# Norm weights asked for ahead of the inputs, input tiles scaled ahead of older norms, a weight unit in its own buffer, and a second home for the bias of odd head pairs

## The chip, the cores and the metric

The kernel runs on one core of one Trainium2 chip. The metric is the device time of one execution, in microseconds (us); lower is better. Engines: PE (TensorE), DVE (VectorE), ACT (ScalarE), POOL (GpSimd), SP (SyncE, which here only issues transfers). ACT issues transfers too.

## The reference

One step of a two-layer decoder over 8 sample tokens and a prompt of 1024 tokens, model width 1024, everything in float32. Cut to what matters here:

```python
h = rms_norm(x, norm_mix[0])                    # x * rsqrt(mean(x^2) + eps) * gain
z = h @ w_in                                    # (1032, 1024) @ (1024, 3080)
qa, ka = rms_norm(z_q), rms_norm(z_k)           # per head of 64, 8 heads
logf = log_sigmoid(z_f + b_f)
qb, kb = partial_rope(rms_norm(...), pos)       # second group of 8 heads
c = cumsum(logf)
s = q @ k.T * SCALE + (c_q - c_k), causal       # heads 0..7: bias of the forget gate
s = q @ k.T * SCALE, three dilated windows      # heads 8..15
o = softmax(s) @ v
x = x + concat(o) @ w_out
x = x + swiglu(rms_norm(x)); x = x + gmlp(rms_norm(x)); x = x + swiglu(rms_norm(x))
```

## The kernel before

The engines' programs are written out by hand, each in the order in which its engine runs it, and tied by semaphores. Nothing is reordered by a scheduler.

**Split products.** A float32 product is made of three fast ones: each matrix is split into a high part, rounded (`Wh`, `Xh`), and a remainder (`Wl`, `Xl`), and PE computes high by high, high by low and low by high. Weights come in units of 128 partitions by 1024 values: a unit is loaded into one of two buffers `raw` (`load_unit`), rounded to `Wh` and its remainder subtracted to `Wl` (on POOL in `split_unit`, on ACT and POOL in `round_unit` and `remainder_unit`), into one of six slots. `split_done` counts the units whose split is done, and the load of unit n waits until unit n - 2 is split, since it takes that unit's buffer.

**Input projection, first pass.** The 1032 tokens lie in nine tiles: tile 0 has the 8 sample tokens, tiles 1 to 8 have 128 each. The pass over layer 0's first group makes three column blocks c = 0, 1, 2 (queries, keys, values), each from four weight units; for each tile, PE does 24 matmuls of 512 columns (`wide_products`, lines 527 to 529). During block 0 the input tiles are also prepared, each through this chain:

- SP loads the tile (`load_input`, line 2095, four buffers `xs`); PE transposes it with eight matmuls (`input_transpose`, line 547); ACT squares it and sums the squares (`input_square`, line 573).
- DVE multiplies the transposed tile by the norm weights `gains` into one of two buffers `hx` (`input_scale`, lines 604 and 607).
- ACT rounds it to `Xh` (`input_high`, line 586) and copies the transposed input to `xT` (`input_copy`, line 580); POOL, for tiles 0 and 1 DVE, subtracts the remainder `Xl` (`input_low`, line 558).

Two tiles are prepared before the loop. In the loop, step tt prepares tile tt + 3 (`inputs_behind`; step 0 prepares tiles 2 and 3). In the same step DVE finishes the norm and rotary part of the products of tile tt: a sum over squares made by ACT (line 752), a reciprocal after ACT's root (lines 691 and 758), two multiplications (761, 764) and four small rotary operations (770, 771, 772, 774). ACT stores tile tt - 1 before it goes on with step tt (`in_store`, line 669), which makes it wait for DVE's last operation on that tile.

The four units of block 0 are loaded by ACT into `raw[0]`, `raw[1]` and two more buffers `raw_first[2]`, `raw_first[3]`; ACT rounds them (line 706) and POOL subtracts (line 2168). Unit 4 (the forget gate's) and unit 5 are split by POOL between input tiles, units 6, 7 and 8 are rounded by ACT (line 382) in step 7 and finished by POOL (line 387). Block 1 begins with units 5 to 8.

**Attention.** Eight pairs of heads, eight query tiles each (units of work; the longest first, `unit(u)`), the steps numbered u. Pairs 0 to 3 add a bias row read from memory (`bias`, 128 partitions by 2 heads by 1024 values), pairs 4 to 7 a constant `dist` in the same place. PE computes scores, DVE adds the bias and takes the row's least value (line 1357), ACT takes the exponential (1274), PE transposes (1160) and multiplies by the values (1188). A row longer than 512 is done in two chunks: columns 512 up first, then columns 0 to 511. PE's `spread_sums` (line 1172) needs DVE's reciprocal of a step (line 1365), which stands behind the second chunk of the unit ahead. The bias of the next pair is loaded by ACT in three parts, issued at steps 2, 4 and 6 of a pair (`load_bias`, lines 1002 and 1004): columns 512 to 1023, 256 to 511, 0 to 255, each as soon as the last reader of these columns of the old pair is done. In between, keys and values of the sample tokens are streamed through `kring` and `ring`, and DVE sums their products (line 1384).

After attention come the output projection, two feed-forward stages and the gated layer, all bound by PE's matmuls.

Of the kernel before, what the change touches and what calls it, by code (L numbers as in the profile page):

```python
# [13 lines left out]
P = 128  # L14
# [20 lines left out]
RAW = 2  # L35
# [57 lines left out]
def build(nc, a):  # L93
    with ExitStack() as ctx:
# [32 lines left out]
        xT = place("xT", [P, KT, T])  # L127
        Xh = place("Xh", [P, KT, T], F32R)
# [130 lines left out]

        used[0] = lfp_memory  # L260
# [29 lines left out]
        raw_first_in = sems("raw_first_in", 2)  # L290
        xt_ps, xt_act = sem("xt_ps"), sem("xt_act")
# [86 lines left out]
        def round_unit(act, n):  # L378

            wait_released(act, n - SPL)  # L380
            act.wait_ge(raw_in[n % RAW], raw_value(n, n))
            act.activation(Wh[n % SPL][:, :], raw[n % RAW][:, :], ACT.Copy).then_inc(split_high, 1)

        def remainder_unit(pool, n):

            pool.wait_ge(split_high, n + 1)
            pool.tensor_tensor(Wl[n % SPL][:, :], raw[n % RAW][:, :], Wh[n % SPL][:, :].bitcast(F32),  # L387
# [128 lines left out]
        def wide_products(pe, n0, s0, tt, bank, first, final):  # L516
# [3 lines left out]
            for k in range(KT):  # L520
                if first and k % 2 == 0:

                    pe.wait_ge(split_done, n0 + k // 2 + 1)
# [64 lines left out]
        def input_act(act, tt):  # L588
            input_high(act, tt)
# [81 lines left out]
        def in_act(act):  # L671
            def step(i):
                for c in range(3):
                    for tt in range(TT):
# [46 lines left out]
        def in_dve(dve):  # L721
            def step(i):
                for c in range(3):
                    if is_first(i) and c == 2:
                        forget_sums_out(dve)
                    for tt in range(TT):
# [14 lines left out]
                        if c == 2:  # L741
# [6 lines left out]
                            continue  # L748
                        dve.wait_ge(z_squared, n + 1)
# [247 lines left out]
        def load_bias(eng, it, part):  # L997
# [1302 lines left out]
```

## Time and profile before

| | us |
|---|---|
| median of 3 runs | 2718.53 (2715.62 to 2722.75) |
| the profiled execution | 2714.44 |
| its span in the profile | 2712.6 |
| PE busy | 2604.7 (96%) |
| DVE busy | 1142.4 (42%) |
| POOL busy | 1114.5 (41%) |
| ACT busy | 547.0 (20%) |
| mean granted TensorE clock | 0.984 |

How to read it: the profile shows one execution. A row of the timeline gives the start, the duration, the engine, the line of the kernel, the operation, what it writes and reads, how often, and in brackets how long the engine had been idle and what ended that. The clock is given as a share of 2.4 GHz.

### The profile page before, as it was taken

How to read it: one execution, taken by the hardware profiler on the slowest of the kernel's cores; microseconds unless marked ns; L12 is line 12 of the kernel's file. 1: busy time of each engine (PE TensorE's matmuls, PEld its weight loads, DVE VectorE, ACT ScalarE, POOL GpSimd, SP SyncE). 2: the span in 40 equal slices, each digit the busy share in tenths (PEclk: the TensorE clock that was granted, in tenths of full speed). 3: DMA queues.
4: the chain of work that ended last, by engine and by line, in shares of the span. 5: the costliest groups of instructions: out<-in, count | busy, mean ns of one | idle time of the engine just before them, and what ended most of it. 6: DMA issues, size and time to landing. Idle time of an engine off the chain costs nothing.

```text
span 2712.6 us, 43122 instructions
## 1 busy us (share of the span) xinstructions
PE 2604.7 (96%) x16505; PEld 2366.2 (87%) x16505; DVE 1142.4 (42%) x2249; ACT 547.0 (20%) x1247; POOL 1114.5 (41%) x714
## 2 busy tenths in 40 slices
PE   7999988998899999999999998998999999999999
PEld 5777755565699999999999986798999999999999
DVE  6636536566516333333333342334533333333333
ACT  5201135565413000000000042311210000000001
POOL 5225115455566433333333254416553333333330
PEclk9999999999999999999999999999999999999999
DMA  5223147575411111111111101101021111111111
GB/s 147 74 77 87 56 123 220 175 215 177 129 55 47 55 47 46 46 46 46 46 46 46 39 32 47 48 16 55 20 67 47 46 46 46 46 46 46 46 31 63
DMA packets 220765, 189.86 MB, mean 70 GB/s; under 512 B 29571, under 2 KB 173443, under 8 KB 220644
## 3 DMA queue, kind: packets, MB, share of 16 engines
q1 hardware_dynamic: 200996, 161.89, 20.4%
q10 hardware_dynamic: 19648, 26.35, 2.7%
q8 instruction: 77, 1.26, 0.2%
q14 instruction: 44, 0.36, 0.0%
HBM read 171.19 MB, written 17.01 MB: 69 GB/s over the span
## 4 chain that ended last, share of the span: by engine, by line
PE 66%; DVE 4%; POOL 1%; ACT 1%; issue 1%; ACTq 0%; POOLq 0%; DVEq 0%
PE ps L495 62%; DVE hs L454 1%; PE ps L527 1%; PE ps L528 1%; PE ps L529 1%; POOL acc_sq L425 1%; ACT ps L1938 1%; DVE Xl L2013 0%; DVE acc_sq L446 0%; PE ps L1913 0%; DVE Xl L468 0%; POOL Xl L468 0%; POOL Wl L387 0%; DVE VM_LATE L2026 0%; PE ps L2050 0%
## 5 line engine op out<-in xcount | busy, mean ns | idle before, releaser
L495 PE MATMUL ps<-Xh,Wh 128*128 128x256 f32 (+2 forms) x2712 | 875.4, 323 | 16.7 <-DVE Xl L2013 6.3
L495 PE MATMUL ps<-Xl,Wh 128*128 128x256 f32 (+2 forms) x2712 | 869.4, 321 | 0.0
L495 PE MATMUL ps<-Xh,Wl 128*128 128x256 f32 (+2 forms) x2712 | 868.0, 320 | 0.0
L373 POOL TENSOR_TENSOR Wh<-raw,zeros 128x1024 fp32r<-128x1024 f32 x178 | 353.3, 1985 | 1076.4 <-PE ps L495 790.1
L495 PEld LDWEIGHTS ps<-Xh,Wh 128*128 128x128 f32 x2712 | 512.2, 189 | 22.9 <-issue 9.5
L495 PEld LDWEIGHTS ps<-Xl,Wh 128*128 128x128 f32 x2712 | 512.0, 189 | 1.2 <-issue 0.6
L495 PEld LDWEIGHTS ps<-Xh,Wl 128*128 128x128 f32 x2712 | 512.5, 189 | 0.0
L376 POOL TENSOR_TENSOR Wl<-raw,Wh 128x1024 fp32r<-128x1024 f32 x178 | 439.2, 2467 | 14.0
L1729 DVE TENSOR_TENSOR Hl<-hf,Hh 128x392 fp32r<-128x392 f32 (+1 forms) x132 | 180.6, 1368 | 466.1 <-ACT Hh L1657 466.1
L495 PE MATMUL ps<-Hh,Wh 128*128 128x392 f32 (+2 forms) x1056 | 341.5, 323 | 2.5 <-DVE xT L1738 2.5
L495 PE MATMUL ps<-Hl,Wh 128*128 128x392 f32 (+2 forms) x1056 | 338.6, 321 | 0.0
L495 PE MATMUL ps<-Hh,Wl 128*128 128x392 f32 (+2 forms) x1056 | 337.4, 319 | 0.0
L1738 DVE TENSOR_TENSOR xT<-ps,xT 128x392 f32<-128x392 f32 (+2 forms) x528 | 262.9, 513 | 168.7 <-PE ps L495 165.7
L1649 ACT ACTIVATE sg<-ps 128x392 f32<-128x392 f32 (+1 forms) x132 | 60.6, 459 | 1068.3 <-PE ps L495 1068.3
L527 PE MATMUL ps<-Wh,Xh 128*128 128x512 f32 (+1 forms) x576 | 231.2, 401 | 22.0 <-ACT VM_EARLY L1929 5.3
L529 PE MATMUL ps<-Wh,Xl 128*128 128x512 f32 (+1 forms) x576 | 229.5, 398 | 0.0
L528 PE MATMUL ps<-Wl,Xh 128*128 128x512 f32 (+1 forms) x576 | 229.1, 398 | 0.0
L1727 DVE TENSOR_TENSOR hf<-ps,sg 128x392 f32<-128x392 f32 (+1 forms) x132 | 67.2, 509 | 324.6 <-PE ps L495 320.5
L495 PEld LDWEIGHTS ps<-Hh,Wh 128*128 128x128 f32 x1056 | 199.6, 189 | 3.5 <-DVE xT L1738 3.2
L495 PEld LDWEIGHTS ps<-Hh,Wl 128*128 128x128 f32 x1056 | 200.2, 190 | 0.0
L495 PEld LDWEIGHTS ps<-Hl,Wh 128*128 128x128 f32 x1056 | 200.1, 190 | 0.0
L1089 POOL TENSOR_TENSOR kring<-kring,qrep 128x512 f32<-128x512 f32 (+1 forms) x96 | 120.8, 1274 | 110.5 <-DMA qrep<-q_sample 48.0
(213 smaller groups left out, 2482.2 us busy)
## 6 DMA issues: line engine op xcount, KB each, us to landing
raw<-in_w_gate_up SPq DMA_DIRECT2D x88, 512.0 KB, 3.8
raw<-in_w_down SPq DMA_DIRECT2D x44, 512.0 KB, 3.5
kring<-in_cache_a_k SPq DMA_DIRECT2D x64, 256.0 KB, 3.7
ring<-in_cache_a_v SPq DMA_DIRECT2D x64, 256.0 KB, 3.4
raw<-in_w_in_even SPq DMA_DIRECT2D x21, 512.0 KB, 4.0
raw<-in_w_in_c SPq DMA_DIRECT2D x16, 512.0 KB, 3.9
xs<-in_x_prompt SPq DMA_DIRECT2D x8, 512.0 KB, 5.7
q_prompt<-zt ACTq DMA_DIRECT2D x16, 256.0 KB, 2.0
```

The costliest lines, as they stand in the source:

```text
L373: pool.tensor_tensor(h[:, :], r[:, :], zeros[:, :].to_broadcast([P, 1024]), ALU.add).then_inc(split_high, 1)
L376: pool.tensor_tensor(l[:, :], r[:, :], h[:, :].bitcast(F32), ALU.subtract).then_inc(split_done, 1)
L425: pool.tensor_tensor(acc_sq[b][:, 0:n], sq[t % 2][:, 0:n], other, ALU.add).then_inc(s["summed"].sem, 1)
L495: ins = nc.tensor.matmul(out, w, x, start=(j == 0), stop=(j == len(pairs) - 1))
L527: nc.tensor.matmul(out, xh, h, start=(k == 0), stop=False)
L528: nc.tensor.matmul(out, xh, l, start=False, stop=False)
L529: last = nc.tensor.matmul(out, xl, h, start=False, stop=(k == KT - 1))
L1089: pool.tensor_tensor(keys, keys, qrep[0:r, g, :], ALU.mult).then_inc(prod_done, 1)
L1649: act.activation(sg[:, k % NB, 0:w], ps[:, gate_bank(i, is_last, k), 0:w], ACT.Silu).then_inc(f["silu"].sem, 1)
L1727: dve.tensor_tensor(hf[:, k % NB, 0:w], ps[:, bank, 0:w], sg[:, k % NB, 0:w], ALU.mult).then_inc(f["hid"].sem, 1)
L1729: dve.tensor_tensor(Hl[:, t, c0:c0 + w], hf[:, k % NB, 0:w], Hh[:, t, c0:c0 + w].bitcast(F32), ALU.subtract).then_inc(f["low"].sem, 1)
L1738: dve.tensor_tensor(x, ps[:, jobs.index(("dn", b, m, 0)) % 6, 0:w], x, ALU.add).then_inc(f["dn_add"].sem, 1)
```

## The change

In words: (1) SP asks for the first norm weights before input tile 1, not after it. (2) At the start, DVE does tile 0 whole, then the remainder of weight unit 1 (POOL did that), then tile 1; ACT rounds tile 0 and unit 1 before it squares tile 1, and unit 2 before it rounds tile 1. (3) In the loop, DVE scales the coming input tile before it sums the squares of tile tt, and ACT rounds that input tile before the root. (4) The load of unit 5 and of unit 8 moves ahead of input tiles 6 to 8, and unit 8 goes into `raw_first[2]`, so that it no longer waits for unit 6. (5) The bias of pairs 1 and 3 lies in `bias_odd`, in memory of `Xh` that is free until pair 4 writes it; so the bias of each further pair, or `dist`, is loaded in one piece at step 2.

```diff
+        bias_odd = nc.alloc_sbuf_tensor_at("bias_odd", [P, 2, SEQ], F32, offset=(xh_memory + 31) // 32 * 32 + 4 * T * (KT // 2))
...
         def round_unit(act, n):
 
             wait_released(act, n - SPL)
-            act.wait_ge(raw_in[n % RAW], raw_value(n, n))
-            act.activation(Wh[n % SPL][:, :], raw[n % RAW][:, :], ACT.Copy).then_inc(split_high, 1)
+            if n == 8:
+                act.wait_ge(raw_first_in[0], 32)
+            else:
+                act.wait_ge(raw_in[n % RAW], raw_value(n, n))
+            act.activation(Wh[n % SPL][:, :], early_home(n)[:, :], ACT.Copy).then_inc(split_high, 1)
...
         def input_act(act, tt):
-            input_high(act, tt)
             input_copy(act, tt)
...
+                        behind = inputs_behind(tt) if is_first(i) and c == 0 else ()
+                        for t in behind[:-1]:
+                            input_high(act, t)
+                            input_act(act, t)
+                        for t in behind[-1:]:
+                            input_high(act, t)
                         if c < 2:
                             act.wait_ge(z_sum, n + 1)
...
-                        if is_first(i) and c == 0:
-                            for t in inputs_behind(tt):
-                                input_act(act, t)
+                        for t in behind[-1:]:
+                            input_act(act, t)
...
             input_square(act, 0)
             round_first(0)
-            input_square(act, 1)
             input_high(act, 0)
             round_first(1)
+            input_square(act, 1)
+            round_first(2)
             input_high(act, 1)
-            round_first(2)
             round_first(3)
...
+                        if is_first(i) and c == 0:
+                            for t in inputs_behind(tt):
+                                input_scale(dve, t)
+                            if tt == 0:
+                                dve.wait_ge(const_in, 16 * CONSTS)
                         dve.wait_ge(z_squared, n + 1)
...
-                        if is_first(i) and c == 0:
-                            for t in inputs_behind(tt):
-                                input_scale(dve, t)
                         dve.wait_ge(z_root, n + 1)
...
             input_scale(dve, 0)
+            input_low(dve, 0)
+            dve.wait_ge(split_high, 2)
+            dve.tensor_tensor(Wl[1][:, :], raw_first[1][:, :], Wh[1][:, :].bitcast(F32), ALU.subtract).then_inc(unit1_low, 1)
             input_scale(dve, 1)
-            input_low(dve, 0)
             input_low(dve, 1)
-            dve.wait_ge(const_in, 16 * CONSTS)
...
-            positive_wait(eng, s_biased, 2 * chunk_base[max(8 * (it - 1) + (4, 6, 8)[part], 0)])
+        def load_bias(eng, it):
+
+            positive_wait(eng, s_biased, 2 * chunk_base[8 * (it - 1)])
             if it < PAIRS // 2:
-                eng.dma_start(bias[:, :, lo:hi], c_dram[2 * it:2 * it + 2, lo:hi].partition_broadcast(P)).then_inc(bias_in[part], 16)
+                eng.dma_start(bias_home(it)[:, :, :], c_dram[2 * it:2 * it + 2, :].partition_broadcast(P)).then_inc(bias_in[0], 16)
...
-                    if j in (2, 4, 6):
-                        load_bias(act, it + 1, (j - 2) // 2)
+                    if j == 2:
+                        load_bias(act, it + 1)
...
                 sp.dma_start(ident[:, :], a["c_ident"]).then_inc(ident_in, 16)
-                load_input(1)
                 sp.dma_start(gains[:, 0, :], a["norm_mix"][0].rearrange("(m p) -> p m", p=P)).then_inc(gain_in, 16)
-                load_input(2)
-                load_input(3)
+                for tt in range(1, NX):
+                    load_input(tt)
...
             load_unit(sp, BASE_FG, BASE_FG, rows(a["w_in_even"], 0, KT, 3 * DH, P), KT)
+            load_unit(sp, 5, 5, rows(a["w_in_even"], 0, 2, DH, DH), 2)
+            with nc.allow_non_contiguous_dma("512-byte and longer runs"):
+                sp.dma_start(raw_first[2][:, :].rearrange("p (a b) -> p a b", a=2), rows(a["w_in_even"], 6, 2, DH, DH)).then_inc(raw_first_in[0], 16)
             for tt in range(6, TT):
                 load_input(tt)
...
-            for n in range(4):
+            for n in (0, 2, 3):
 
                 pool.wait_ge(split_high, n + 1)
+                if n == 3:
+                    pool.wait_ge(unit1_low, 1)
+                pool.tensor_tensor(Wl[n][:, :], raw_first[n][:, :], Wh[n][:, :].bitcast(F32), ALU.subtract).then_inc(
+                    split_done, 2 if n == 2 else 1)
```

How the order moves, at three places. First ACT before the loop (`hx_117` belongs to even tiles, `hx_118` to odd ones; `Wh_65` to `Wh_68` are weight units 0 to 3). Before:

```order
L573 ACTIVATE hx_117,ssx<-xs_88 8x1024
L706 ACTIVATE Wh_65<-raw_63 128x1024
L573 ACTIVATE hx_118,ssx<-xs_89 128x1024
L586 ACTIVATE Xh<-hx_117 128x8x8
L706 ACTIVATE Wh_66<-raw_64 128x1024
L586 ACTIVATE Xh<-hx_118 128x8x128
L706 ACTIVATE Wh_67<-raw_first_115 128x1024
L706 ACTIVATE Wh_68<-raw_first_116 128x1024
```

ACT before the loop now:

```order
L585 ACTIVATE hx_117,ssx<-xs_88 8x1024
L722 ACTIVATE Wh_65<-raw_63 128x1024
L598 ACTIVATE Xh<-hx_117 128x8x8
L722 ACTIVATE Wh_66<-raw_64 128x1024
L585 ACTIVATE hx_118,ssx<-xs_89 128x1024
L722 ACTIVATE Wh_67<-raw_first_115 128x1024
L598 ACTIVATE Xh<-hx_118 128x8x128
L722 ACTIVATE Wh_68<-raw_first_116 128x1024
```

The square of tile 1, which needs tile 1's transfer, moved behind the first two units.

Second, DVE in step 1 of block 0, before (`zsq` are the squares of tile 1's products, `hx_117` is input tile 4):

```order
L752 TENSOR_REDUCE ss<-zsq_96 128x8
L604 TENSOR_SCALAR eps_ms<-ssx 128x1
L607 TENSOR_TENSOR hx_117<-ps,gains 128x1024
L758 RECIPROCAL zrs<-zstd 128x8
L761 TENSOR_TENSOR zt_93<-ps,zrs 128x512
```

DVE in the same step now:

```order
L615 TENSOR_SCALAR eps_ms<-ssx 128x1
L618 TENSOR_TENSOR hx_117<-ps,gains 128x1024
L773 TENSOR_REDUCE ss<-zsq_96 128x8
L776 RECIPROCAL zrs<-zstd 128x8
L779 TENSOR_TENSOR zt_93<-ps,zrs 128x512
```

The input's scaling stands ahead of the sum, and the reciprocal directly behind it.

Third, SP's transfers behind the constants, before (`raw_63`, `raw_64` are the two weight buffers, `xs` are input tiles 4 to 8):

```order
L2095 DMA xs_88<-in_x_prompt 128x1024
L2095 DMA xs_89<-in_x_prompt 128x1024
L312 DMA raw_63<-in_w_in_even 128x8x128
L2095 DMA xs_90<-in_x_prompt 128x1024
L2095 DMA xs_91<-in_x_prompt 128x1024
L2095 DMA xs_88<-in_x_prompt 128x1024
L312 DMA raw_64<-in_w_in_even 128x2x512
```

SP's transfers at that place now:

```order
L2120 DMA xs_88<-in_x_prompt 128x1024
L2120 DMA xs_89<-in_x_prompt 128x1024
L316 DMA raw_63<-in_w_in_even 128x8x128
L316 DMA raw_64<-in_w_in_even 128x2x512
L2145 DMA raw_first_115<-in_w_in_even 128x2x512
L2120 DMA xs_90<-in_x_prompt 128x1024
L2120 DMA xs_91<-in_x_prompt 128x1024
```

Two units of 512 KB each stand ahead of tile 6, and the second of them has a buffer of its own.

## Rows read from the trace of the kernel before

**Rows 1.** Windows: busy us (x instructions) of the five engines, clock, DMA share, GB/s

```profile
62.00:96.00 34.00, 26.01 (x98) 18.78 (x99) 23.48 (x42) 11.93 (x19) 15.90 (x7) 0.85 0.32 100
96.00:360.00 264.00, 260.74 (x1184) 201.59 (x1182) 134.64 (x261) 27.91 (x58) 67.06 (x31) 1.00 0.24 70
360.00:750.00 390.00, 345.75 (x3110) 228.46 (x3110) 229.58 (x782) 210.73 (x555) 195.10 (x237) 0.96 0.60 180
750.00:2712.60 1962.60, 1921.53 (x11877) 1879.67 (x11875) 715.02 (x1114) 265.34 (x569) 803.95 (x422) 0.99 0.15 45
```

**Rows 2.** Waits of PE, 0 to 120 us: total, times, longest

```profile
PE ps L527 <- POOL Xl L558: 4.3, 1, 4.3
PE ps L527 <- POOL Wl L387: 4.0, 2, 3.7
```

**Rows 3.** Timeline of the start, 0 to 22 us

```profile
8.08 1.06 ACT L573 ACTIVATE hx<-xs 128x1024 f32<-128x1024 f32 x1 [1.64 <-DMA xs<-in_x_prompt]
10.85 0.14 DVE L604 TENSOR_SCALAR eps_ms<-ssx 8x1 f32<-8x1 f32 x1 [9.94 <-DMA gains<-in_norm_mix]
13.44 2.46 DVE L558 TENSOR_TENSOR Xl<-hx,Xh 128x1024 fp32r<-128x1024 f32 x1 [1.00 <-ACT Xh L586]
14.78 5.70 POOL L2168 TENSOR_TENSOR Wl<-raw_first,Wh 128x1024 fp32r<-128x1024 f32 x2
21.92 1.91 PE L547 MATMUL ps<-ident,xs 128*128 128x128 f32 x16
```

**Rows 4.** Timeline of block 0: one step, a free rotary operation, PE's wait

```profile
43.63 0.67 DVE L752 TENSOR_REDUCE ss<-zsq 128x8 f32<-128x512 f32 x1
44.28 1.21 DVE L607 TENSOR_TENSOR hx<-ps,gains 128x1024 f32<-128x1024 f32 x1
...
46.67 2.65 POOL L558 TENSOR_TENSOR Xl<-hx,Xh 128x1024 fp32r<-128x1024 f32 x1 [3.11 <-ACT Xh L586]
47.09 2.39 DVE L770 TENSOR_TENSOR rope_u<-zt,cs 128x128 f32<-128x128 f32 x1
...
49.99 0.68 DVE L752 TENSOR_REDUCE ss<-zsq 128x8 f32<-128x512 f32 x1
...
65.98 0.80 PE L527 MATMUL ps<-Wh,Xh 128*128 128x512 f32 x1 [4.34 <-POOL Xl L558]
...
75.80 0.29 DVE L770 TENSOR_TENSOR rope_u<-zt,cs 128x128 f32<-128x128 f32 x1
```

**Rows 5.** Timeline of PE and ACT where block 1 begins

```profile
79.60 0.39 PE L529 MATMUL ps<-Wh,Xl 128*128 128x512 f32 x1
79.83 0.39 PE L527 MATMUL ps<-Wh,Xh 128*8 128x512 f32 x1
...
84.79 1.06 ACT L382 ACTIVATE Wh<-raw 128x1024 fp32r<-128x1024 f32 x1 [5.62 <-DMA raw<-in_w_in_even]
...
88.32 0.41 PE L527 MATMUL ps<-Wh,Xh 128*8 128x512 f32 x1 [3.66 <-POOL Wl L387]
...
89.61 0.63 PE L528 MATMUL ps<-Wl,Xh 128*8 128x512 f32 x1
90.03 0.63 PE L529 MATMUL ps<-Wh,Xl 128*8 128x512 f32 x1
```

**Rows 6.** Waits of DVE, 340 to 760 us: total, times, longest

```profile
DVE S L1357 <- DMA bias<-c_dram: 7.8, 3, 3.1
DVE S L1357 <- DMA dist<-in_c_dist: 0.9, 1, 0.9
```

**Rows 7.** Timeline of PE at the first two changes of the head pair

```profile
417.84 0.44 PE L1172 MATMUL ps<-ident,rl 128*64 128x128 f32 x4 [2.57 <-DVE rl L1365]
...
464.45 0.70 PE L1172 MATMUL ps<-ident,rl 128*64 128x128 f32 x4 [2.87 <-DVE rl L1365]
```

**Rows 8.** Transfers by line: times, KB each, median us to landing

```profile
bias<-c_dram ACTq DMA_DIRECT2D x6, 256.0 KB, 4.7
```

**Rows 9.** Waits of POOL, 395 to 560 us: total, times, longest

```profile
POOL kring L1089 <- DMA qrep<-q_sample: 28.6, 4, 8.7
```

More of the change, by code:

```diff
@@ L127, in build @@
         xT = place("xT", [P, KT, T])
+        xh_memory = used[0]
         Xh = place("Xh", [P, KT, T], F32R)
@@ L290, in build @@
         raw_first_in = sems("raw_first_in", 2)
+        unit1_low = sem("unit1_low")
         xt_ps, xt_act = sem("xt_ps"), sem("xt_act")
@@ L380, in round_unit, with early_home @@
             wait_released(act, n - SPL)
-            act.wait_ge(raw_in[n % RAW], raw_value(n, n))
-            act.activation(Wh[n % SPL][:, :], raw[n % RAW][:, :], ACT.Copy).then_inc(split_high, 1)
+            if n == 8:
[3 more added lines that the diff above has]
+            act.activation(Wh[n % SPL][:, :], early_home(n)[:, :], ACT.Copy).then_inc(split_high, 1)
+        def early_home(n):
+            return raw_first[2] if n == 8 else raw[n % RAW]
         def remainder_unit(pool, n):
             pool.wait_ge(split_high, n + 1)
-            pool.tensor_tensor(Wl[n % SPL][:, :], raw[n % RAW][:, :], Wh[n % SPL][:, :].bitcast(F32),
+            pool.tensor_tensor(Wl[n % SPL][:, :], early_home(n)[:, :], Wh[n % SPL][:, :].bitcast(F32),
                                ALU.subtract).then_inc(split_done, 1)
@@ L520, in wide_products @@
             for k in range(KT):
-                if first and k % 2 == 0:
+                if first and k == 2 and isinstance(n0, int) and n0 == 0:
+                    pe.wait_ge(unit1_low, 1)
+                elif first and k % 2 == 0:
                     pe.wait_ge(split_done, n0 + k // 2 + 1)
@@ L995, in cached_rows, with bias_home, load_first_bias @@
             return sp.dma_start(dst[0:r], src)
-        def load_bias(eng, it, part):
+        def bias_home(it):
+            return bias if it % 2 == 0 else bias_odd
+        def load_first_bias(eng, part):
             lo, hi = PARTS[part]
-            positive_wait(eng, s_biased, 2 * chunk_base[max(8 * (it - 1) + (4, 6, 8)[part], 0)])
+            eng.dma_start(bias[:, :, lo:hi], c_dram[0:2, lo:hi].partition_broadcast(P)).then_inc(bias_in[part], 16)
+        def load_bias(eng, it):
+            positive_wait(eng, s_biased, 2 * chunk_base[8 * (it - 1)])
             if it < PAIRS // 2:
-                eng.dma_start(bias[:, :, lo:hi], c_dram[2 * it:2 * it + 2, lo:hi].partition_broadcast(P)).then_inc(bias_in[part], 16)
+                eng.dma_start(bias_home(it)[:, :, :], c_dram[2 * it:2 * it + 2, :].partition_broadcast(P)).then_inc(bias_in[0], 16)
             elif it == PAIRS // 2:
-                eng.dma_start(dist[:, lo:hi], a["c_dist"][:, lo:hi]).then_inc(bias_in[part], 16)
+                eng.dma_start(dist[:, :], a["c_dist"][:, :]).then_inc(bias_in[0], 16)
         def pair_values(it, lo, hi):
@@ L1044, in att_sp @@
                 for part in range(3):
-                    load_bias(sp, 0, part)
+                    load_first_bias(sp, part)
                 for g in range(2):
@@ L1345, in biased @@
                 if qt == 7 and (it <= PAIRS // 2):
-                    for part in ((0,), (1, 2))[c]:
+                    for part in ((0,), (1, 2))[c] if it == 0 else (0,):
                         dve.wait_ge(bias_in[part], 16 * (it + 1))
@@ L1351, in biased @@
                 for h in range(2):
-                    row = bias[:, h, c0:c1] if it < PAIRS // 2 else dist[:, SEQ - n + c0:SEQ - n + c1]
+                    row = bias_home(it)[:, h, c0:c1] if it < PAIRS // 2 else dist[:, SEQ - n + c0:SEQ - n + c1]
                     least = mx if last else mx_tail
@@ L2124, in project @@
                     for j in range(IN_UNITS):
-                        if is_first(i) and c == 0:
+                        n = 1 + 4 * c + j
+                        if is_first(i) and (c == 0 or n in (5, 8)):
                             continue
-                        n = 1 + 4 * c + j
+                        if is_first(i) and n == 10:
+                            sp.wait_ge(split_done, 9)
+                            sp.sem_inc(raw_in[0], 16)
                         src = a["w_in_even"][2 * j * P:(2 * j + 2) * P, bass.ds(i * (3 * DH + HEADS) + c * DH, DH)]
```

1 line of the change is left out of this document (removed).

## The prediction

> **What bounds the kernel now.** I read the busy time by stretches first [rows 1]: from 96 to 360 us and from 750 us to the end PE is busy 98 to 99% of the time at a clock near 1, so nothing that the change touches can be gained there; a PE that reaches 96 us or 750 us earlier carries the whole gain to the end. Two stretches are left. From 62 to 96 us PE is busy 26.0 of 34 us at a mean clock of 0.85, and in attention 346 of 390. Then the waits of PE at the beginning [rows 2]: 4.3 us for the remainder of an input tile, 3.7 us for that of a weight unit. Then the timelines: what stands in front of PE's first long run [rows 3], how long a step of block 0 takes on DVE [rows 4], why unit 8 is late [rows 5], and in attention who waits for the bias [rows 6, 7].
>
> **The start.** I count from 21.92 us, where tile 0's products end [rows 3], and call it E. DVE idles until 10.85 us for the norm weights, though tile 1 landed by 8.08 us [rows 3]; their transfer came 2.8 us behind it in the same queue. Now it goes first. It may land soon after the identity, some 5 to 8 us, or as late as now; tile 1 may land as late as 10.85, since the same bytes are ahead of both. I take 9.3 and 10.8. PE transposes tile 1 before tile 0's products, so these begin at about 12.8 (before 12.5). The four remainders were serial on POOL, the last ending at 14.78 + 5.70 = 20.48 [rows 3]. Now POOL does three; DVE does unit 1 at about 11 us, when POOL is idle. ACT squares tile 1 (1.25 us with the read of its sum) from 10.9, rounds unit 2 until 13.2, tile 1 until 15.2, unit 3 until 16.1. A remainder costs POOL about 2.4 us (two took 5.70, of which 1.1 us went to waiting for DVE) and DVE about 1.1 (13.44 + 2.46 = 15.90, begun when POOL's second ended at 14.8) [rows 3]. So POOL's unit 2 runs 13.2 to 15.6, DVE's tile 1 until 16.6, POOL's unit 3 until 19.0; six products follow, 1.4 us, so E is 20.5. **Gain 1.4 us**; bounds -0.5 (tile 1 still later, at 12.7) and +3.5 (it lands at 8.5).
>
> DVE and POOL block each other: the remainder on DVE took 2.46 us beside POOL's [rows 3], and a rotary operation 2.39 us against 0.29 when POOL was idle [rows 4]. The Trainium skill (SBUF — State Buffer, Who interferes with whom) states this as an exclusive lock held for a whole instruction; it speaks against giving DVE a remainder of POOL's, since two remainders never run side by side. By it the start would gain about a microsecond less if the two met. The trace agrees that they exclude each other, and in my order they don't meet.
>
> **Block 0.** DVE's step is 49.99 - 43.63 = 6.36 us [rows 4], and 10.1 us in the steps where POOL also splits unit 4 or 5. PE's step is less: 24 matmuls 0.23 us apart [rows 5] and eight transposes, about 6.5 us. So DVE falls behind by some 3.6 us in each long step, until PE waits 4.34 us for tile 7 [rows 4]. The step ends when POOL's remainder releases the lock: sum of squares 0.6, scaling 1.2, rounding 1.1, and POOL starts at 46.67, 3.04 us after the step's start. Without the sum ahead it starts about 2.4 us after it. The sum now stands behind the scaling and the root behind the rounding, which delays DVE's reciprocal to 2.75 us after the start (before 1.8), but then come only two multiplications (1.4 us) before the rotary part, which waits for POOL anyway. **Each step is 0.6 us shorter.** Step 0 instead ends about 0.5 us later after E (ACT rounds and copies two tiles ahead of its root). With four steps before tile 7, its remainder is done at E + 42.0 (before E + 44.0), while PE wants it at E + 39.6 as before: the wait falls from 4.3 to 2.3 us, 2 us gained.
>
> The clock: after the wait of 4.34 us products start 0.43 us apart (1.2 GHz) for about 14 matmuls, as later at 89.61 and 90.03 against 79.60 and 79.83 [rows 5]: 14 x 0.2 = 2.8 us. In attention a wait of 2.57 us left the clock at 2.4 GHz, matmuls of L1172 taking 0.44; one of 2.87 us brought 0.70, the low level [rows 7]. A wait of 2.3 us should keep it. **Gain 4.8 us**; bounds 2.0 (clock falls all the same) and 6.9 (wait gone).
>
> **Block 1.** Unit 8 waited for unit 6's buffer: ACT could round it only at 84.79, after 5.62 us of waiting for its transfer [rows 5], and PE's product started at 88.32 after 3.66 us, then ran at 1.2 GHz until about 92. Now it is in place long before. ACT rounds 6, 7, 8 in a row from about E + 52.3, POOL subtracts at 2.4 us each until E + 60.5, and PE, which is at block 1 at E + 53.1, waits about 1 us for each of the three: 3.2 us in all, where it lost 0.4 + 3.7 + about 1.9 by the clock. **Gain 2.7 us**; bounds 1 (three short waits bring the clock down) and 5. The two early loads, 1 MB, go ahead of tile 6, which PE transposes some 20 us later: nothing. The manual count on SP and the removed load are hidden likewise; with no cover, a load late by 4 us would cost its lateness.
>
> **Attention.** At three changes of pair DVE waits for the last quarter of the bias, 7.8 us, and 0.9 us for `dist` [rows 6], since it is asked for at step 6, used in the same step, and takes 4.7 us to land [rows 8]. PE stands behind it for 2.57, 2.87 and more [rows 7], at 1.2 GHz afterwards for about 3 us in two cases. All parts are now asked for at step 2, four steps ahead; a pair's eight steps take 464.45 - 417.84 = 46.6 us [rows 7], four of them over 12 us even where they are short, against 4.7 us for a quarter of the bytes. So 8.7 us of waits go; the better clock may give 1.5 more, and the key loads that queue behind 1 MB at once, with the next wait of the kind for `qrep`, may take as much back. **Gain 8.7 us**; bounds 3 and 11. Fewer issues on ACT, eight by 0.4 us, are hidden by its idle time (busy 211 of 390 us).
>
> **Sum.** 1.4 + 4.8 + 2.7 + 8.7 = 17.6 us off the profiled execution's 2714.4: 2696.8. That execution lies 4.1 us under the median of 2718.5; against the median the forecast is **2700.9 us**.
>
> **Rivals.**
> 1. The clock falls again in blocks 0 and 1, since the shortened waits are still waits. For it: after 2.87 us it fell. It takes 2.8 + 1 us back: 2704.7.
> 2. The attention gain moves into another wait: POOL already waits 28.6 us for `qrep` [rows 9], and DVE's key sums follow POOL. That slack hardly showed on PE; if it takes 6 of the 8.7 us, the result is 2706.9.
> 3. The beginning gives nothing: the norm weights, 128 x 8 values of 4 bytes each, spread in the queue before tile 1 and delay tile 1 by more than they come earlier (in the rows they took 2.8 us behind tile 1). Only attention is left: 2709.8. The Trainium skill (DMA: Bandwidth & Descriptors, Rules for kernel authors) says that a last dimension with a stride becomes one descriptor per element; that makes this transfer 1024 small ones. The trace agrees in so far as 4 KB took 2.8 us longer than the 512 KB before it. Whether they now delay tile 1 as long, no row shows.
> 4. Slower: the 1 MB bias at step 2 holds back the key and value loads in the same 16 DMA engines, whose share averages 0.60 over attention [rows 1]; DVE's sums then wait for POOL's products and PE for DVE. Four bursts; to lose over 8 us in all it must cost (17.6 + 8.2) / 4 = 6.5 us each, more than the 4.7 us that a load takes from issue to landing [rows 8]: 2727 at the least. Against it: the old part 0, half as large, at the same step caused no wait.
> 5. The change does not do what it says: `bias_odd` lies in `Xh`, and if its load had to wait for something of the projection, pair 1 would stall. It waits for nothing before pair 2. I give it no chance of its own.
>
> **How the numbers follow.** Forecast 0.60, rival 1 0.18, rival 2 0.12, rival 3 0.08, rival 4 0.02. The forecast's own bounds, not all at one end, give gains of 12 to 24 us. The range reaches from 2693 to 2711: at the upper end it takes in rivals 1 to 3, at the lower a gain of 25 us or runs that lie nearer to the profiled one. A measurement here can tell 0.3%, 8.2 us, from no change. Forecast and rival 1 are faster by more, three quarters of rival 2 and a quarter of rival 3: 0.89. Within 0.3%: 0.09. Slower: 0.02.
>
> **What would show it.** Right: tile 0's products end near 20.5 us; DVE's short step in block 0 is about 5.8 us; PE waits 2 to 2.5 us for tile 7 with the clock at 1; no wait above 1.5 us at unit 8; block 1's first forget product starts 9 us earlier; no wait of DVE for `bias` or `dist` behind pair 0; attention is 8 to 9 us shorter between its first score and its last. Wrong: tile 1 landing after 12 us, a low clock in 60 to 70 us, DVE waiting for POOL's key products after step 2 of a pair, or new waits of PE for `ring` after 417 us.

## The result and the profile after

| | before | after |
|---|---|---|
| median, us | 2720.64 (2715.62 to 2723.99, 4 runs) | 2696.78 (2690.29 to 2700.66, 4 runs) |
| the profiled execution | 2714.44 | 2700.66 |
| its span | 2712.6 | 2698.8 |

The ratio is 0.9911, with a 95% interval of 0.9885 to 0.9937: faster by 0.9%, 23.9 us between the medians (17 to 31 us by the interval). The profiled executions differ by only 13.8 us, since that of before was one of the faster of its kernel and that of after the slowest of its four. The table follows PE through the profiled executions, in us from the start of the span.

| start of | before | after | gained by then | forecast |
|---|---|---|---|---|
| the transposes behind tile 0's products | 21.92 | 20.86 | 1.1 | 1.4 |
| block 1 | 79.83 | 76.63 | 3.2 | 6.2 |
| the first forget product | 90.46 | 85.69 | 4.8 | 8.9 |
| attention's first transposes | 367.27 | 362.23 | 5.0 | 8.9 |
| the output projection | 737.01 | 722.23 | 14.8 | 17.6 |

From there to the end it was 1975.6 and 1976.6 us: as the prediction said, nothing is gained there. Attention itself took 369.7 us before and 360.0 after.

The windows of after, cut where those of [rows 1] are, a little earlier at the later borders (busy us of PE, PE's weight loads, DVE, ACT, POOL, then clock, DMA share, GB/s):

```profile
62.00:96.00 34.00, 28.80 (x120) 20.74 (x120) 28.00 (x50) 10.62 (x20) 16.34 (x7) 0.95 0.26 80
96.00:350.00 254.00, 251.28 (x1144) 194.60 (x1145) 129.56 (x250) 27.18 (x57) 65.84 (x30) 1.00 0.24 70
350.00:740.00 390.00, 350.76 (x3151) 233.09 (x3150) 231.65 (x783) 210.09 (x555) 199.09 (x239) 0.97 0.61 182
```

PE is busy 28.8 us of the 34 behind 62 us, where it had been 26.0 at a lower clock. The waits of PE between 0 and 120 us, against [rows 2]:

```profile
PE ps L539 <- POOL Xl L570: 3.4, 1, 3.4
PE ps L539 <- POOL Wl L398: 3.0, 3, 1.2
```

The start, against [rows 3]:

```profile
10.05 0.14 DVE L615 TENSOR_SCALAR eps_ms<-ssx 8x1 f32<-8x1 f32 x1 [9.14 <-DMA gains<-in_norm_mix]
...
11.29 0.69 PE L559 MATMUL ps<-ident,xs 128*128 128x128 f32 x2 [4.80 <-DMA xs<-in_x_prompt]
...
11.59 1.23 DVE L797 TENSOR_TENSOR Wl<-raw,Wh 128x1024 fp32r<-128x1024 f32 x1 [0.72 <-ACT Wh L722]
...
15.65 1.50 DVE L570 TENSOR_TENSOR Xl<-hx,Xh 128x1024 fp32r<-128x1024 f32 x1 [1.12 <-ACT Xh L598]
...
16.64 2.77 POOL L2201 TENSOR_TENSOR Wl<-raw_first,Wh 128x1024 fp32r<-128x1024 f32 x1 [0.57 <-ACT Wh L722]
```

The norm weights came only 0.8 us earlier, and tile 1 came later: it is transposed from 11.29, where it had landed by 8.08. Unit 1's remainder takes DVE 1.23 us while POOL is idle. The last two rows meet: DVE's remainder of tile 1 ends at 17.15, 0.5 us into POOL's, and POOL's takes 2.77 us.

One step of block 0 on DVE, and the wait of PE, against [rows 4]:

```profile
42.72 0.14 DVE L615 TENSOR_SCALAR eps_ms<-ssx 128x1 f32<-128x1 f32 x1
...
45.16 2.41 POOL L570 TENSOR_TENSOR Xl<-hx,Xh 128x1024 fp32r<-128x1024 f32 x1 [2.77 <-ACT Xh L598]
...
45.55 0.69 DVE L779 TENSOR_TENSOR zt<-ps,zrs 128x512 f32<-128x512 f32 x1
...
46.27 1.84 DVE L782 TENSOR_TENSOR zt<-zt,gqk 128x512 f32<-128x512 f32 x1
...
48.15 0.29 DVE L788 TENSOR_TENSOR rope_u<-zt,cs 128x128 f32<-128x128 f32 x1
...
48.96 0.15 DVE L615 TENSOR_SCALAR eps_ms<-ssx 128x1 f32<-128x1 f32 x1
...
63.85 0.50 PE L539 MATMUL ps<-Wh,Xh 128*128 128x512 f32 x1 [3.38 <-POOL Xl L570]
...
64.71 0.63 PE L539 MATMUL ps<-Wh,Xh 128*128 128x512 f32 x1
```

The step is 48.96 - 42.72 = 6.24 us; before it was 6.36. POOL starts 2.44 us after the step's start, as forecast, but now holds back the multiplication by the head gains: 1.84 us, where it takes 0.69 without POOL. It ends at 48.11, 0.5 us behind POOL's remainder. The rotary operation behind it has its free 0.29. PE waits 3.38 us, and 0.9 us behind that its products take 0.63: the low clock.

Where block 1 begins, against [rows 5]:

```profile
77.50 1.04 ACT L389 ACTIVATE Wh<-raw_first 128x1024 fp32r<-128x1024 f32 x1
...
79.17 0.40 PE L539 MATMUL ps<-Wh,Xh 128*8 128x512 f32 x1 [1.01 <-POOL Wl L398]
...
81.52 0.40 PE L539 MATMUL ps<-Wh,Xh 128*8 128x512 f32 x1 [0.79 <-POOL Wl L398]
...
84.29 0.40 PE L539 MATMUL ps<-Wh,Xh 128*8 128x512 f32 x1 [1.22 <-POOL Wl L398]
```

ACT rounds unit 8 without waiting for its transfer. PE waits three times for about 1 us, 3.02 us in all (forecast 3.2), and keeps its clock. In attention (waits between 340 and 760 us, against [rows 6]):

```profile
PE ps L1197 <- DVE rl L1390: 5.6, 8, 1.5
...
DVE S L1382 <- DMA bias<-c_dram: 2.0, 1, 2.0
```

The one wait for bias left is pair 0's. PE's waits for `rl` fell from 13.4 to 5.6 us, the longest from 3.9 to 1.5.

### The profile page after: what moved, and what is told of

It reads as the page before. It is cut to its first block, busy times and chain, and to the rows that moved or that the text cites. A ratio compares the mean times of both kernels' runs of the same rounds, so it can differ in the third digit from the quotient of the medians.

```text
span 2698.8 us, 43111 instructions
## 1 busy us (share of the span) xinstructions
PE 2597.8 (96%) x16505; PEld 2361.6 (88%) x16505; DVE 1140.9 (42%) x2250; ACT 544.3 (20%) x1247; POOL 1109.1 (41%) x713
## 4 chain that ended last, share of the span: by engine, by line
PE 65%; DVE 4%; POOL 2%; ACT 1%; issue 1%; ACTq 0%; POOLq 0%; DVEq 0%
PE ps L506 62%; DVE hs L465 1%; PE ps L539 1%; PE ps L541 1%; PE ps L540 1%; DVE acc_sq L457 1%; POOL acc_sq L436 1%; ACT ps L1963 1%; DVE Xl L479 1%; DVE Xl L2038 1%; POOL Xl L479 0%; PE ps L1938 0%; POOL Wl L398 0%; PE ps L2075 0%; DVE VM_EARLY L2028 0%
## 5 line engine op out<-in xcount | busy, mean ns | idle before, releaser
L506 PEld LDWEIGHTS ps<-Xh,Wh 128*128 128x128 f32 x2712 | 511.9, 189 | 23.4 <-issue 9.2
```

The costliest lines, as they stand in the source:

```text
L506: ins = nc.tensor.matmul(out, w, x, start=(j == 0), stop=(j == len(pairs) - 1))
```

## The experiments

Milestones are those of the table above; each kernel is given by its median and its ratio to before in the same comparison. Its milestones come from one profiled execution. How far those scatter can be read off kernels that have the same instructions up to a milestone: block 1 starts at 76.02, 76.46, 76.63 and 77.42 us in four executions of the changed beginning, and at 78.87 and 79.83 in two of the old one. The first product of tile 7, counted from the transposes behind tile 0's products (E, as in the prediction), scatters by less than 0.1 us.

**The bias alone**, on the kernel before:

```diff
-                    if j in (2, 4, 6):
-                        load_bias(act, it + 1, (j - 2) // 2)
+                    if j == 2:
+                        load_bias(act, it + 1)
```

together with `bias_home`, as in the change; nothing of its other parts.

> Part 5 of the change alone on the kernel before: the bias of pairs 1 and 3 in its second home, each further bias in one piece at step 2. If the attention term is right and independent of the beginning: DVE waits for bias or dist at most in pair 0, PE's waits at line 1172's matmuls of the pair changes fall from 2.6, 2.9, 3.9 and 1.8 us to under 1.6, the stretch from the first attention transposes to the first output projection (369.7 us before, 360.0 in the changed kernel) is 360 us, and the whole is 9 to 10 us faster than before. Rival, that the shift at the beginning is what helped attention to meet its loads: the stretch stays over 365 us.

Measured: 2702.32 us against 2719.7 for before (0.9939, 0.9919 to 0.9959), 17.4 us, more than the 9 to 10 expected. Block 1 begins at 78.87 and attention at 367.94, about where they did; attention takes 356.6 us.

```profile
PE ps L1181 <- DVE rl L1374: 5.2, 8, 1.2
DVE S L1366 <- DMA bias<-c_dram: 2.0, 1, 2.0
```

So this part does not need the others, and is worth about twice the 8.7 us that the prediction gave it (11 to 22 us by the interval).

**The beginning alone**: the change without `bias_odd`, with the three loads at steps 2, 4 and 6.

> The changed kernel with part 5 undone: the beginning alone. By the profile of the changed kernel: attention begins 5.0 us earlier than before (362.2), its stretch is again 369 to 370 us, and the whole is 5 us faster than before. Rival, that the profiled execution understates the beginning (medians differ by 24 us, profiles by 14): attention begins at or before 359 us and the whole is 10 us or more faster.

Measured: 2713.71 (0.9977, 0.9963 to 0.9991), 6.0 us. Attention starts at 361.82, 5.4 us earlier than before, but takes 376.0 us. In this execution DVE's waits for `bias` were 9.9 us (pair 0's among them) and for `dist` 1.5. The two parts add up: 17.4 + 6.0 = 23.4 against 23.9 measured.

**The old order in the loop**: the change without its part 3.

```diff
+                        if is_first(i) and c == 0:
+                            for t in inputs_behind(tt):
+                                input_scale(dve, t)
                         dve.wait_ge(z_root, n + 1)
```

(and ACT's counterpart, as before).

> The changed kernel with part 3 undone: in the loop the sum stands again ahead of the scaling, the root ahead of the rounding. Lock theory (the remainder on POOL now starts before DVE's second multiplication, line 782, reads its two SBUF operands, so that multiplication waits for POOL's end too, 1.84 us for 0.69): the new order is worth 0.1 us a short step; undone, a short step of DVE is 6.36 us with a multiplication of 0.69, PE's wait for tile 7 is 3 to 4.5 us, and block 1 begins within 1 us of the changed kernel's 76.6 us. The theory of the prediction (each step 0.6 us shorter, 2 us in all): block 1 begins 2 us or more later, at 78.6 or after.

Measured: 2700.28 (0.9921, 0.9901 to 0.9941), not to be told from the change by time. PE waits 4.30 us for tile 7 (3.38 with the new order). Tile 7's first product starts at E + 44.0 us in this execution and in the five others with the old order, at E + 43.0 in the four with the new one. But block 1 starts only 0.7 us later (77.30), which is within the scatter, and the forget product 0.2 us later (85.90). DVE's step:

```profile
42.26 0.67 DVE L764 TENSOR_REDUCE ss<-zsq 128x8 f32<-128x512 f32 x1
...
45.72 2.38 DVE L782 TENSOR_TENSOR rope_u<-zt,cs 128x128 f32<-128x128 f32 x1
...
48.62 0.68 DVE L764 TENSOR_REDUCE ss<-zsq 128x8 f32<-128x512 f32 x1
```

The old order gives POOL's time to the rotary operation, the new one to the multiplication ahead of it; the step is 6.36 or 6.24 us. What the reordering does is mainly to let the last remainder start 0.6 us sooner after the start of its step, once.

**Units 4 and 5 rounded on ACT**, on the changed kernel, so that POOL has one pass over them, not two:

```diff
                 if tt in (4, 6):
-                    split_ahead(pool, BASE_FG + (tt - 4) // 2)
+                    remainder_unit(pool, BASE_FG + (tt - 4) // 2)
...
                             input_act(act, t)
+                        if is_first(i) and c == 0 and tt in (1, 3):
+                            round_unit(act, BASE_FG + (tt - 1) // 2)
```

> The changed kernel, but units 4 and 5 are rounded by ACT in steps 1 and 3 (ACT idles over 5 us in both), POOL makes only their remainders. Lock theory: the long steps are long because two further POOL operations hold off DVE's small operations; one of 2.35 us less makes each long step 1.9 to 2.4 us shorter (10.0 to about 7.8), DVE's step is then near PE's 6.5 and the wait of 3.4 us for tile 7 and the low clock after it go: block 1 begins 5 us or more earlier, 71.6 or before, the whole 4 to 6 us faster than the changed kernel. Rival, that PE's wait is set by the input chain of short steps: the wait stays over 2 us and block 1 begins after 74.

Measured: 2695.06 (0.9907, 0.9889 to 0.9925). Two waits for tiles are left:

```profile
60.41 0.50 PE L539 MATMUL ps<-Wh,Xh 128*128 128x512 f32 x1 [0.29 <-POOL Xl L570]
66.63 0.50 PE L539 MATMUL ps<-Wh,Xh 128*128 128x512 f32 x1 [0.41 <-POOL Xl L570]
```

The granted clock is 1.00 from 62 to 96 us, block 1 starts at 72.28, 4.3 us before the changed kernel's. DVE does the same work as there: what held PE was the length of DVE's steps beside POOL. The whole gained less than expected: the median is 1.7 us under the changed kernel's, not 4 to 6, which the times cannot tell apart. The forget product starts at 82.19, 3.5 us earlier; PE now waits 3.9 us for the remainders of units 6 to 8, where it waited 3.0.

**Unit 8 alone** (part 4) and **the start alone** (parts 1 and 2), each on the kernel before.

> Part 4 alone on the kernel before: units 5 and 8 loaded ahead of tile 6, unit 8 in its own buffer. If unit 8's late transfer is all that block 1 gains from, tile 0's products end at 21.9 us and block 1 starts at 79.8 us as before, the idle time of ACT for the transfer of unit 8 goes, PE's wait of 3.66 us there falls to about 1 us and its first forget product starts 4 to 5 us earlier, at 85.5 to 86.5 us; attention keeps its 368 to 376 us. Median 3 to 5 us under before (ratio 0.998 to 0.999). Rival: the three remainders on POOL become the bound and PE waits as long for them: first forget product later than 88 us and less than 2 us gained.

Measured: 2717.12 (0.9985, 0.9973 to 0.9996). The transposes and block 1 start as before (22.00, 79.70), the forget product at 87.35, 3.1 us earlier; the longest wait there is 1.2 us. The theory of the late transfer held in kind, but had promised 4 to 5 us; the rival, a first forget product later than 88 us, falls.

> Parts 1 and 2 alone on the kernel before: gains first, unit 1's remainder on DVE. If the start's gain is carried through block 0, tile 0's products end at 20.5 to 20.9 us, PE's wait for tile 7 stays near 4.3 us, block 1 starts 1 to 1.5 us earlier than before (78.3 to 78.8), and its first forget product 0 to 1.5 us earlier. Rival: block 1's end is set by the transfer of unit 8, which hangs on unit 6's split, and so moves along with the start too; then the forget product also comes 1 to 1.5 us earlier. If the transfer hangs on the queue alone, nothing is left of the gain at the forget product (90.3 or later). Median within 0.1% of before.

Measured: 2717.53 (0.999, 0.998 to 1.0001). Transposes at 20.59; tile 7's first product at 64.62, 1.4 us earlier than before, after the same wait of 4.34 us. Block 1 starts at 77.39, earlier than expected, since 8 products behind that wait were slow (0.58 us or more) where it was 13 before. The forget product starts at 89.24, 1.2 us earlier. ACT waits 5.38 us for the transfer of unit 8 as it did before (5.62), and that transfer comes 1.6 us earlier: it moves along with the start, as the rival in the expectation had it.

**The bias asked for later**: the changed kernel with `j == 6`, and with `j == 4`, in place of `j == 2`.

> The changed kernel with the bias of the next pair asked for at step 6 instead of step 2, still in one piece and with its second home. If the time of asking is what counts, DVE waits again for bias at each change of pair, longer than before since the piece has four times the last part's bytes: 4 to 7 us each, 15 to 25 us in all, and attention takes 372 to 380 us; median 12 to 20 us above the changed kernel, about the time before or worse. If the one piece and the missing waits for readers of the old pair did it, attention stays under 365 us.

Measured for step 6: 2730.12 (1.0039, 1.0027 to 1.0051), slower than before. Attention takes 391.1 us, more than expected.

```profile
DVE S L1382 <- DMA bias_odd<-c_dram: 15.9, 2, 8.1
DVE S L1382 <- DMA bias<-c_dram: 7.4, 2, 5.5
DVE S L1382 <- DMA dist<-in_c_dist: 5.6, 1, 5.6
```

> The changed kernel with the bias of the next pair asked for at step 4, one piece, second home. Asked for at step 6 it came up to 8.1 us too late. Step 4 is two steps earlier, and the steps behind it took 3.1 to 3.6 us each in the short half of a pair. If lateness just shifts with the time of asking, 8.1 us less 6.5 to 7 us leaves waits of 0 to 1.5 us at the changes of pair, 0 to 4 us in all; attention takes 356 to 364 us and the median lies within 4 us of the changed kernel. If the piece of 1 MB is slow for another reason (its transfer waits behind key loads), waits of 4 us or more remain at each change and attention takes over 370 us.

Measured for step 4: 2697.17 (0.9921, 0.9908 to 0.9934), as with step 2; attention 357.4 us, DVE's only wait for bias 1.5 us, pair 0's. The time of asking decides, not the one piece: at step 6 the piece is up to 8.1 us too late, at step 4 it is in time.

**The norm weights first, alone**, on the kernel before.

```diff
-                load_input(1)
                 sp.dma_start(gains[:, 0, :], ...)
+                load_input(1)
```

> Part 1 alone on the kernel before: the norm weights asked for ahead of input tile 1. DVE can scale tile 0 about 1 us earlier (9.9 to 10.1 us), but tile 1 lands 2 to 3 us later than in before, at about 11.3 us, and ACT squares it before it rounds any unit but the first. If POOL's four serial remainders (2.4 us each) set the end of tile 0's products, these end 2 to 3 us later than before, at 23.5 to 25 us, because the first rounding behind tile 1's square is later. If the square of tile 1 hardly matters, the end stays at 21.5 to 22.3 us. Median within 0.1% of before, or slower by 0.1%.

Measured: 2722.7 (1.0013, 1.0002 to 1.0023). DVE has the norm weights at 9.83, 1.0 us earlier; ACT squares tile 1 at 11.05, 3.0 us later; the transposes start at 22.98, 1.1 us later, between the two expectations. Tile 7's first product is 1.1 us late too:

```profile
67.04 0.79 PE L527 MATMUL ps<-Wh,Xh 128*128 128x512 f32 x1 [4.34 <-POOL Xl L558]
...
70.19 0.47 PE L528 MATMUL ps<-Wl,Xh 128*128 128x512 f32 x1
```

By 70.19 the products are fast again, 3.2 us behind the wait. Before, it took 5.7 us:

```profile
71.69 0.42 PE L528 MATMUL ps<-Wl,Xh 128*128 128x512 f32 x1
```

So block 1 starts at 79.75 not because the delay was made up, but because the clock was low for a shorter time in this execution. The forget product starts at 90.54, as before (90.46).

**DVE subtracts the tiles' remainders too**, on the kernel with ACT's roundings:

```diff
-        X_DVE = 2
+        X_DVE = TT
...
                                           ALU.add).then_inc(z_sum, 1)
+                        if is_first(i) and c == 0:
+                            for t in inputs_behind(tt):
+                                if t > 2:
+                                    input_low(dve, t)
```

> The kernel with ACT rounding units 4 and 5, and besides DVE itself subtracts the remainder of every input tile (behind its sum of squares), so POOL has only two weight remainders in block 0. If the two engines exclude each other, taking POOL's 2.4 us out of DVE's step is worth more than the 1.1 us that DVE takes on: its step is about 5.6 to 5.9 us, never behind PE's 6.5, the multiplication by the head gains takes 0.7 us and the first rotary operation 0.3 in every step without a weight remainder, PE waits for no tile's remainder, and block 1 starts at or before 72.3 us. If DVE's rows are slow for another reason (DVE just has too much work), the step grows by 1.1 us to about 7.4 and PE waits for tiles: block 1 later than 75 us.

Measured: 2693.13 (0.9896, 0.9883 to 0.9909). DVE took on 1.23 us of work per step, and its step shrank:

```profile
37.90 2.41 POOL L398 TENSOR_TENSOR Wl<-raw,Wh 128x1024 fp32r<-128x1024 f32 x1 [18.84 <-ACT Wh L389]
...
37.93 2.45 DVE L798 TENSOR_TENSOR rope_w<-zt,cs 128x64 f32<-128x64 f32 x1
...
40.63 0.15 DVE L615 TENSOR_SCALAR eps_ms<-ssx 128x1 f32<-128x1 f32 x1
...
43.04 1.23 DVE L570 TENSOR_TENSOR Xl<-hx,Xh 128x1024 fp32r<-128x1024 f32 x1 [0.54 <-ACT Xh L598]
...
45.13 0.69 DVE L790 TENSOR_TENSOR zt<-zt,gqk 128x512 f32<-128x512 f32 x1
...
46.20 0.22 DVE L798 TENSOR_TENSOR rope_w<-zt,cs 128x64 f32<-128x64 f32 x1
...
46.66 0.15 DVE L615 TENSOR_SCALAR eps_ms<-ssx 128x1 f32<-128x1 f32 x1
```

The first two rows are the only meeting of the two engines in this stretch: an operation that takes 0.22 us in the next step takes 2.45 beside POOL's 2.41. The step without POOL is 46.66 - 40.63 = 6.03 us (expected 5.6 to 5.9; 6.25 with ACT's roundings alone). PE waits for no tile, and block 1 starts at 71.69, 0.6 us earlier than with ACT's roundings alone, less than the scatter. The rival, that DVE simply has too much work, falls: its step did not grow. The times do not tell the two kernels apart.

**DVE subtracts units 6 to 8 too**, on top of that: first behind tile 8's sum, then one step earlier.

```diff
+                            if tt == TT - 1:
+                                dve.wait_ge(split_done, 6)
+                                for unit in ACT_UNITS:
+                                    remainder_unit(dve, unit)
```

> The kernel in which DVE subtracts the remainder of every input tile, and besides it subtracts those of units 6 to 8 where POOL did (1.2 us each and alone, 2.4 us and in a row on POOL). DVE stood idle there for 3.0 us. If PE's waits of 2.0, 0.5 and 0.2 us at block 1 come from POOL's pace, they fall to 1.0 to 1.5 us in all, and the first forget product starts at 79.5 to 80.5 us (before this step 81.7); attention unchanged, median 1 to 2 us under that kernel. If PE's waits come from ACT's roundings, nothing is gained.

Measured: 2697.7 (0.9923, 0.991 to 0.9936). They stood in the wrong step: DVE reached that place late, and PE stood still.

```profile
79.55 0.59 PE L539 MATMUL ps<-Wh,Xh 128*8 128x512 f32 x1 [6.09 <-DVE Wl L398]
```

> The remainders of units 6 to 8 on DVE as in the run before, but one step earlier, in tile 7's step instead of tile 8's: there DVE waited 3.0 us for the root behind ACT's three roundings, here it subtracts meanwhile. Behind tile 8's sum they started at 78.3 us, 5 to 6 us after they could. If place is all that was wrong, the first starts at 72.7 us, PE waits 1 to 2 us in all at block 1, and the first forget product starts at 79.5 to 80.5 us (with POOL's remainders 81.7); median 2690 to 2694. If DVE's own norm work then becomes late and PE waits for it in block 1 instead, the forget product is at 82 or later and the median no better than 2694.

With `TT - 2`: 2691.14 (0.9897, 0.9878 to 0.9915), the lowest median of the study, 5.6 us under the changed kernel's; their ratios' intervals overlap, and the ratio is no better than the 0.9896 of the kernel in which DVE subtracts the tiles' remainders alone, so the profile carries the claim more than the times.

```profile
72.64 2.36 DVE L398 TENSOR_TENSOR Wl<-raw,Wh 128x1024 fp32r<-128x1024 f32 x2 [1.02 <-ACT Wh L389]
74.92 1.22 DVE L398 TENSOR_TENSOR Wl<-raw_first,Wh 128x1024 fp32r<-128x1024 f32 x1
```

```profile
62.00:96.00 34.00, 32.02 (x149) 24.43 (x148) 26.72 (x56) 9.22 (x17) 4.63 (x2) 1.00 0.23 72
```

PE waits 0.9 us at block 1, is busy 32.0 of the 34 us, and starts the forget product at 78.09 and attention at 354.71, 7.5 us before the changed kernel. That is more than expected (79.5 to 80.5).

## Why the prediction was right, and where it was not

**The total** was right: 2700.9 forecast, 2696.8 measured, inside the range, and the sign with it. The gain was forecast at 17.6 us, from a median of 2718.5 for before, and measured at 23.9, from 2720.6 with one more run. It came that near because two errors of size went opposite ways: the beginning gave 5 to 6 us where 8.9 were forecast, the bias 17.4 where 8.7 were. That is partly luck.

**The start** (1.4 forecast, 1.1 measured) held in its steps: the weights 0.75 us later than taken (10.05), tile 1 0.5 us later, the rest in the order given. "In my order they don't meet" was not quite so: the two remainders met for 0.5 us. Parts 1 and 2 together gain 1.3 us here, and part 1 alone costs 1.1; part 2 alone was not run, so it stays open whether it would give more without part 1. Rival 3's mechanism exists: with the norm weights ahead of it, tile 1 is read 3.0 us later. The Trainium skill (DMA: Bandwidth & Descriptors, Rules for kernel authors) says that a last dimension with a stride becomes one descriptor per element, which would make this transfer 1024 pieces; no view of these runs counts them. The rival does not decide, since of the 3.0 us only 1.1 reach the transposes.

**Block 0** (4.8 forecast; 3.20 - 1.06 = 2.1 measured) is where the prediction failed, at the step "each step is 0.6 us shorter". It had DVE's two multiplications run free before POOL's lock. The second one reads and writes SBUF alone, and it met POOL's remainder: it could end only behind it. POOL's earlier start was thus paid back in the same step, 6.24 us for 6.36. Counted from E, step 0 cost 0.3 us, the three steps behind it gave 0.4 together, the 0.6 us came once, in the step that makes tile 7's remainder, and that remainder took POOL 2.36 us for 2.67. So tile 7's first product came 1.0 us sooner (E + 43.0 for E + 44.0), and the wait shrank from 4.34 to 3.38 us, not to 2.3. By the prediction's own signs the short step should have been 5.8 us and the clock 1. The first multiplication reads PSUM; it took 0.69 us with POOL's remainder running (45.55 to 46.24 against 45.16 to 47.57). The Trainium skill (SBUF — State Buffer, Who interferes with whom) says that a DVE instruction with two inputs in SBUF contends with a POOL instruction that reads SBUF, and that one with at most one such input, in its plain mode, does not. The trace agrees on both multiplications. The prediction quoted the section for the start and did not carry it through to this operation.

**The clock**: rival 1 came true in block 0. After 3.38 us the clock fell. Windows of 4 us, first of before, then of after:

```profile
64.00:68.00 4.00, 2.02 (x5) 1.65 (x6) 3.96 (x7) 1.92 (x5) 1.92 (x1) 0.61 0.19 73
68.00:72.00 4.00, 4.00 (x12) 3.13 (x11) 3.83 (x5) 2.65 (x4) 2.37 (x1) 0.53 0.05 20
```

```profile
64.00:68.00 4.00, 4.00 (x11) 3.15 (x12) 3.20 (x9) 1.50 (x3) 0.36 (x1) 0.57 0.17 66
68.00:72.00 4.00, 4.00 (x18) 3.22 (x18) 3.81 (x7) 1.33 (x3) 2.05 (x1) 1.00 0.00 0
```

PE did 12 matmuls in the second window before, 18 after. The 2.1 us gained in block 0, less 1.0 us of wait, leave 1.1 us at the clock, of the 2.8 that were charged to it. But the runs do not show this to be a gain of the change. Behind the wait of 4.3 us, 13, 12, 8, 8, 7 and 7 products were slow in the six executions with the old order; behind the wait of 3.4 us, 13, 8, 7 and 6 in the four with the new one. Before happened to be profiled with 13, after with 7. In block 1 the clock of after stayed high through three waits of 1 us.

**Block 1** (2.7 forecast): unit 8's transfer no longer matters, and the three waits are as forecast. From block 1's start to the forget product it is 10.6 us before and 9.1 after, 1.6 us, but since the start of block 1 scatters, that understates it. Counted from E, the forget product starts at 68.5 us before (67.6 to 68.8 in the three other executions with unit 8 in its old place), at 65.3 with part 4 alone and with the old order in the loop, and at 64.8 in all four executions that have the new order too. So part 4 gives 3.2 us and the new order 0.5: in those four, block 1 itself starts anywhere from 55.6 to 56.8, and PE waits off what it is early at POOL's remainders of units 6 to 8.

**Attention** (8.7 forecast) had the right mechanism, in place and time: no wait behind pair 0, and waits back as soon as the load is asked for late. Its size was off: 9.7 us between the profiled executions, 17.4 us between medians. The term was read from one execution, a short one. In the five profiled executions with the old loading (before, the beginning alone, unit 8, the start, the norm weights) attention takes 369.7, 376.0, 375.3, 380.6 and 384.1 us; in the eight with the bias asked for at step 2 or 4, 356.6 to 363.1. Three of them, before, the norm weights alone, and after:

```profile
367.27:737.01 369.74, 330.45 (x3033) 214.50 (x3033) 224.08 (x754) 209.67 (x553) 181.30 (x229) 0.97 0.61 182
367.15:751.21 384.06, 342.00 (x3032) 220.50 (x3033) 223.92 (x754) 210.29 (x553) 181.27 (x229) 0.93 0.59 175
362.23:722.23 360.00, 326.65 (x3032) 211.62 (x3033) 225.04 (x754) 209.03 (x553) 180.67 (x229) 0.98 0.62 187
```

PE does the same matmuls in all of them, so a longer busy time is a lower clock. The means of the five and of the eight are 377.1 and 359.3 us, 17.8 apart: PE is idle for 40.4 and 31.2 us, and busy for 336.7 and 328.1. About 9 us are waits, near the 8.7 forecast; the mis-sized term is "the better clock may give 1.5 more", which measured 8.6. It also makes up most of the scatter among the five: their idle time is 38.1 to 42.6 us, their busy time 330.5 to 342.5.

**Rivals 2 and 4** had nothing: POOL's waits for `qrep` between 395 and 560 us are 29.5 us where they were 28.6 [rows 9], and the loads of 1 MB landed 4.7 and 8.0 us after issue, with no wait of DVE for them. Rival 5 did not occur.

## What to carry to other kernels

When an operation of POOL is moved in time beside DVE, ask which DVE operation stands there next: if it works in SBUF alone, it pays what another one paid before, and the step gets hardly shorter. To take the load off, let DVE do the subtraction itself (1.2 us) rather than wait for POOL to do it (2.4 us); here this made the step 0.2 us shorter, which the times did not show. And what one profiled execution shows behind a wait is a sample: before sizing its removal, look for a second execution, since the low clock behind the wait may vary by more than the wait.

## What the runs showed that I had not expected

The length of a wait does not tell whether the clock falls. The prediction took a bound from two rows, high after 2.57 us and low after 2.87 [rows 7]. The kernel with the start alone has these four changes of pair (timeline of PE; 0.44 is the high level, 0.7 the low one):

```profile
418.34 0.44 PE L1176 MATMUL ps<-ident,rl 128*64 128x128 f32 x4 [3.24 <-DVE rl L1369]
...
468.30 0.69 PE L1176 MATMUL ps<-ident,rl 128*64 128x128 f32 x4 [3.27 <-DVE rl L1369]
...
521.86 0.44 PE L1176 MATMUL ps<-ident,rl 128*64 128x128 f32 x4 [3.68 <-DVE rl L1369]
...
570.23 0.70 PE L1176 MATMUL ps<-ident,rl 128*64 128x128 f32 x4 [2.40 <-DVE rl L1369]
```

High after 3.68 us, low after 2.40: a bound on the wait alone is not there, and the step to "2.3 us should keep it" had no ground. At the start of block 1, in the kernel where DVE subtracts the tiles' remainders, the products were slow 1.2 us behind a wait of 1.97 us.

Also unexpected: moving work to the busier engine made its steps shorter. The prediction had both prices, 1.1 us on DVE and 2.4 on POOL, but kept the remainders of tiles 2 to 8 on POOL.
